# The low parts of the weights: VectorE alone in place of VectorE and GpSimd in turn

## What is computed

```
for l in range(2):                       # first network
    h = x @ w_in[l]                      # 1024 x 3620
    y = [mla(h), stick_breaking(h), forgetting(h), memory(h, mem @ w_mem_kv[l])]
    merged = sum(sigmoid(merge_r @ w_up[n]) * ((y[n] * silu(gate[n])) @ w_branch[l, n]))
    x = layer_norm(ALPHA * x + merged @ w_out[l])
for l in range(2):                       # second network
    z = rmsnorm(x, norm_g[l]) @ w_in_2[l]
    o = [dense A, window B, neighbourhood C, differential D attention of z], each * silu(its gate)
    x = x + concat(o) @ w_out_2[l]
return rmsnorm(x, final_g)
```

## Time and profile before

| | us |
|---|---|
| median of 3 runs | 1549.19 (1547.57 to 1551.87) |
| the profiled execution | 1553.94 |
| span of its trace | 1552.0 |
| PE busy | 1423.3 (92%) |
| VectorE busy | 904.6 (58%) |
| ScalarE busy | 681.2 (44%) |
| GpSimd busy | 366.7 (24%) |

### The profile page before, as it was taken

One profiled execution on the slowest core, in us unless ns is written; L12 is line 12 of the kernel. 1 busy time (PEld: TensorE's weight loads), 2 busy tenths in 40 slices (PEclk: granted clock), 3 DMA queues, 4 the chain that ended last, 5 costly groups with the idle time before them and its releaser, 6 DMA issues.

```text
span 1552.0 us, 21224 instructions
## 1 busy us (share of the span) xinstructions
PE 1423.3 (92%) x8026; PEld 1097.0 (71%) x8026; DVE 904.6 (58%) x1705; ACT 681.2 (44%) x1477; POOL 366.7 (24%) x265
## 2 busy tenths in 40 slices
PE   7999898999989999999998699997999799997997
PEld 7757675877987576767788666665777656664776
DVE  4655437556672554484576565468655466568655
ACT  3544344555233554444552344335444444335443
POOL 2232121245231321222452111410001111310011
PEclk9999999999999999999999799999999899998999
DMA  6412620225333121211263323511213322511211
GB/s 225 109 29 85 158 68 28 62 61 204 109 136 82 29 82 55 82 35 56 67 224 85 93 54 68 116 55 48 93 64 96 82 63 60 116 55 48 96 62 54
DMA packets 191120, 131.72 MB, mean 85 GB/s; under 512 B 91436, under 2 KB 181164, under 8 KB 191020
## 3 DMA queue, kind: packets, MB, share of 16 engines
q1 hardware_dynamic: 179534, 112.29, 26.0%
q10 hardware_dynamic: 11486, 18.09, 3.6%
HBM read 118.03 MB, written 12.32 MB: 84 GB/s over the span
## 4 chain that ended last, share of the span: by engine, by line
PE 68%; DVE 18%; ACT 7%; issue 3%; DMA 2%; ACTq 1%; POOL 0%; DVEq 0%; POOLq 0%
PE pb L1399 18%; PE pb L1400 16%; PE pb L1401 16%; PE pb L1477 5%; PE pb L1421 5%; PE pb L1455 4%; ACT prob L1533 2%; DMA wr<-w_out 2%; ACT wh L1552 2%; ACT tmp L1533 1%; DVE wl L1861 1%; DVE scr L2151 1%; DVE xl L1868 1%; DVE small L2128 1%; PE pb L1439 1%
## 5 line engine op out<-in xcount | busy, mean ns | idle before, releaser
L2296 POOL TENSOR_TENSOR wl<-wr,wh 128x512 fp32r<-128x512 f32 x170 | 236.7, 1392 | 893.8 <-ACT wh L1552 890.1
L1399 PE MATMUL pb<-xh,wl 128*128 128x512 f32 (+1 forms) x832 | 354.0, 425 | 25.1 <-DVE xl L1868 21.9
L1400 PE MATMUL pb<-xl,wh 128*128 128x512 f32 (+1 forms) x832 | 323.6, 389 | 0.0
L1401 PE MATMUL pb<-xh,wh 128*128 128x512 f32 (+1 forms) x832 | 323.2, 388 | 0.0
L1861 DVE TENSOR_TENSOR wl<-wr,wh 128x512 fp32r<-128x512 f32 x200 | 162.9, 815 | 159.3 <-ACT wh L1552 159.0
L1399 PEld LDWEIGHTS pb<-xh,wl 128*128 128x128 f32 x832 | 164.0, 197 | 106.4 <-issue 54.1
L1552 ACT CAST wh<-wr 128x512 fp32r<-128x512 f32 x370 | 211.0, 603 | 50.2 <-PE pb L1401 42.8
L1401 PEld LDWEIGHTS pb<-xh,wh 128*128 128x128 f32 x832 | 163.5, 197 | 32.0
L1400 PEld LDWEIGHTS pb<-xl,wh 128*128 128x128 f32 x832 | 164.8, 198 | 24.3 <-issue 3.8
L1533 ACT ACTIVATE prob<-prob,small 128x512 f32<-128x512 f32 (+3 forms) x128 | 76.2, 597 | 153.0 <-DVE small L2105 143.6
L1455 PE MATMUL pb<-cst,prob 128*128 128x128 f32 x768 | 118.5, 276 | 24.4 <-ACT prob L1533 8.2
(11 more groups left out here) (196 smaller groups left out, 2449.9 us busy)
## 6 DMA issues: line engine op xcount, KB each, us to landing
wr<-w_in SPq DMA_DIRECT2D x39, 1024.0 KB, 5.1
wr<-w_in SPq DMA_DIRECT2D x48, 256.0 KB, 4.6
wr<-w_out SPq DMA_DIRECT2D x10, 1024.0 KB, 5.7
wr<-w_branch SPq DMA_DIRECT2D x48, 128.0 KB, 2.3
x<-prob SPq DMA_DIRECT2D x12, 512.0 KB, 2.6
wr<-w_out SPq DMA_DIRECT2D x48, 128.0 KB, 3.0
wr<-w_mem_kv SPq DMA_DIRECT2D x4, 1024.0 KB, 5.5
prob<-x ACTq DMA_DIRECT2D x2, 2048.0 KB, 10.3
```

What stands on the lines that cost most here:

```text
L1399: e.matmul(ps, ll, rh, start=start, stop=False)
L1400: e.matmul(ps, lh, rl, start=False, stop=False)
L1401: t = e.matmul(ps, lh, rh, start=False, stop=stop)
L2296: t = e.tensor_tensor(wl[:, j % 2, c0:c1], wr[:, j % 2, c0:c1], wh[:, j % 2, c0:c1].bitcast(F32), ALU.subtract)
```

## The change

The step `cast` on VectorE loses its condition that the chunk be even, and GpSimd's branch for odd chunks is taken out, with its semaphore. PE and SyncE wait for the last chunk on the one semaphore that is left. The instruction is the same, with the same tiles; GpSimd keeps its other work. Behind the first hunk the line numbers of the changed kernel are up to 12 smaller (1861 becomes 1858).

```diff
-            c = (upto - 1) // 512
-            w.wait_ge(w_lo, w_lo.at((j, c - c % 2)))
-            if c:
-                w.wait_ge(w_lo2, w_lo2.at((j, c - 1 + c % 2)))
+            w.wait_ge(w_lo, w_lo.at((j, (upto - 1) // 512)))
...
-            elif k == "cast" and s["c"] % 2 == 0:
+            elif k == "cast":
...
-            elif k == "cast" and s["c"] % 2:
-                j, c = s["j"], s["c"]
-                c0, c1 = 512 * c, min(512 * c + 512, WEIGHTS[j][1] * WEIGHTS[j][2])
-                own()
-                w.wait_ge(w_hi, w_hi.at((j, c)))
-                t = e.tensor_tensor(wl[:, j % 2, c0:c1], wr[:, j % 2, c0:c1], wh[:, j % 2, c0:c1].bitcast(F32), ALU.subtract)
-                t.then_inc(w_lo2.sem, w_lo2.mark((j, c)))
...
-                    w.wait_ge(w_lo, w_lo.at((j - 2, c - c % 2)))
-                    w.wait_ge(w_lo2, w_lo2.at((j - 2, c - 1 + c % 2)))
+                    w.wait_ge(w_lo, w_lo.at((j - 2, c)))
```

More of the change, by code:

```diff
@@ L1229, in build @@
     w_lo, a_lo, v_copy, v_att, v_turn, v_fn = (signal(n) for n in ("w_lo", "a_lo", "v_copy", "v_att", "v_turn", "v_fn"))
-    w_lo2, y_lo, p_fn = (signal(n) for n in ("w_lo2", "y_lo", "p_fn"))
+    y_lo, p_fn = (signal(n) for n in ("y_lo", "p_fn"))
     (d_cst, d_tail, d_mem, d_pos, d_par, d_lam, d_z, d_spread, d_res, d_store, d_tab) = (
@@ L1241, in build @@
     SIGNALS = [feat, gemm, logit, turned, heado, aux, w_hi, a_hi, a_copy, a_att, a_turn, a_fn, w_lo, a_lo, v_copy, v_att,
-               v_turn, v_fn, w_lo2, y_lo, p_fn, d_cst, d_tail, d_mem, d_pos, d_par, d_lam, d_z, d_spread,
+               v_turn, v_fn, y_lo, p_fn, d_cst, d_tail, d_mem, d_pos, d_par, d_lam, d_z, d_spread,
                d_res, d_store, d_tab, *d_first, d_par1, *d_x, *d_w, *d_acc, *d_bias]
@@ L2280, in own @@
         def own():
-            w.wait_ge(w_lo2, w_lo2.n)
             w.wait_ge(y_lo, y_lo.n)
```

## The result

| | us | ratio to before (95% interval) |
|---|---|---|
| before, median of 6 runs | 1549.73 (1547.57 to 1552.42) | |
| changed, median of 6 runs | 1559.53 (1554.64 to 1564.57) | 1.006 (1.0035 to 1.0086) |
| changed, the profiled execution and its span | 1561.69, 1559.6 | |

A forecast was written before the change was run, and what follows sets the result against it. PE, busy 1423.3 of 1552.0 us, was taken as the bound, so only its stops count. Terms at known stops sum to plus 3.6 us, new stops add 2: 1549.2 + 5.6 = 1554.8, taken as 1555 us, range 1542 to 1571.

The forecast's parts named there:

- VectorE's work: VectorE's busy time: 904.6 us plus 102 for 170 moved rests, less 49 for collisions, gives 958 us.
- The relief: On VectorE, collisions with GpSimd's rests go: 29 us in the rests and 20 us in other instructions.
- Standing in line: On VectorE, a moved rest waits for ScalarE's cast and delays everything behind it; branch D's copy starts 2.2 us late.
- Branch D's sum: Branch D: 1.1 us late less 0.85 for a collision, about plus 0.25 per layer, bounds minus 1.5 and plus 2.2.
- Branch B: Rotations in branch B, second network: PE also waits for ScalarE, plus 0.9 us twice, 1.8.
- My term for new stops: PE stops not yet in the trace, where its lead is used up: 2 us, ends 0 and 12.
- First network and layer norm: Moved rests before PE's stops at latent and stick-breaking attention add time; collisions gone in layer 1's norm and merge save it.
- Rotations: Second network, PE's wait for line 2197: a moved rest stands right ahead, plus 0.3 us four times, 1.2.
- Relief wins: Rival: VectorE's collisions lie where PE stops, 12.8 us against 4 us of added cost, so 1540 us; chance 0.14.
- absorbed: Rival: the planner's lead swallows both added work and relief, so 1549 to 1552 us; chance 0.19.
- No relief: Rival: GpSimd does not slow VectorE, so 0.6 us is added everywhere, plus 15, 1564 us; chance 0.05.
- Lockstep: Rival: lateness spreads between VectorE and ScalarE through attention stages, plus 18 to 30, 1567 to 1579 us; chance 0.12.

The follow-up runs named there:

- two kernels that differ in it: Kernel without odd rests, TensorE reading high parts, 1522.98 us; the same with 170 odd rests made on GpSimd but not waited for by TensorE, 1547.38 us.
- the pair of traces above: Traces of the changed kernel and of it with 18 second-network rests put behind the next copy or mixing, which measured 1549.24 us, ratio 1.0001 to before.
- second_net: Against the kernel before, odd rests moved to VectorE in the second network only, left on GpSimd in the first: 1558.05 us, ratio 1.0050.
- the half kernel: Against the kernel before, odd rests moved to VectorE in the first network only, left on GpSimd in the second: 1553.70 us, ratio 1.0018.

## Why the prediction was right, point by point

- **VectorE's work.** Forecast 904.6 + 102 - 49 = 958 us; measured 961.5. The relief alone, from two kernels that differ in it, is 55.7 us against my 49; so the moved rests add some 112.6 (56.9 + 55.7) and not 102, and the two errors partly cancel. The mean of the rests was to be near 0.69 and is 0.755: GpSimd's other 86 additions and subtractions collide too; one rest in branch B took 2.47 us. I had said that those collisions stay, and did not look for what would newly stand beside them.
- **Standing in line, the mechanism.** Right, and in branch D right in size on VectorE. The copy was to start 2.2 us late: 2.25 (4.65 against 2.40). The next maxima 1.3 late: they start 8.05 us after the last ones (1071.98 - 1063.93) instead of 6.72. The stop behind line 1830 was to lose 0.85: it fell from 1.6 to 0.8.
- **Branch D's sum.** Wrong, plus 0.25 per layer. The failing step is "1.1 late where PE stands 3.1 us at 1084": I followed the delay only to stops that were in the trace already, by way of ScalarE's exponentials. PE also waits for this copy to leave its bank. Before, the copy ended 0.68 us ahead of the products (1067.62 against 1068.30), now 0.15 ahead, so only 0.53 us of its 2.25 were covered and 1.72 went into the stop. The upper bound that I gave, 2.2, held the stop (1.73 longer) but not the clock behind it; the place costs 4.70 against the kernel with the rest moved. Against the kernel before, PE loses 1.2 us over the whole of branch D in the first layer and 2.0 in the second, where I had 0.25. Some of it returns, because PE arrives later at the stop for the exponentials, 2.1 us at the longest now against 3.1.
- **Branch B.** I had plus 0.9 twice for the rotation. What was found is a new stop of 1.95 us ahead of the value products and, in this trace, the lower clock behind it: PE loses 3.6 and 3.5 us against the kernel before in the two layers. My term for new stops, 2 us with 12 as its end, was to hold all such places; two in B and two in D make up the loss of the second network (12.4 us in the pair of traces above, 8.3 by the medians). The term was mis-sized: by the medians it should have been some 4 us (8.3 less the 4.3 of my other terms for this network), by the traces up to 8 (3.6 + 3.5 + 1.2 + 2.0, less my 1.8 and 0.5 for these branches).
- **First network and layer norm.** My terms for it (latent 1.2, one at 174 of 0.6, stick-breaking 1.0, norm -1.9, merge -1.6) sum to -0.7; measured +3.9, with an interval of 0.2 to 5.4, so a gain of 0.7 is out and the size is open. The stops behind the latent attention grew by 2.8 (line 1474 behind ScalarE's copy, 7.3 to 10.1) where I had 1.2. The norm did not gain: its three rows of waits sum to 13.6 us (6.2 + 4.9 + 2.5), against 8.9 behind line 2080 and 4.3 behind 2072 before.
- **Rotations.** Right: 1.9 to 3.2 us at line 1505, forecast plus 1.2.
- **Rivals.** Relief wins and absorbed are out by the time. No relief had 1564, as far from the 1559.53 as the forecast; what puts it out are the rows, with the rests at 755 ns and the 55.7 us. Absorbed was not far from what the work can do: with 18 rests in another place the whole change is. Lockstep's mechanism, a late copy that makes PE late, was at work in four places, not in sixteen.

So the sign and the mechanism of standing in line were right, and the size, 5.6 against 9.8, was short in two places: in the stops that did not exist yet, with the clock behind them, and in the first network, where -0.7 stands against a measured 3.9 that no trace shows. Part of it is luck. The range, 1542 to 1571, would have held absorbed and no relief too, and 2 of the 5.6 us were a guess with no place named, while the terms that had a place were too low in branch D and branch B.

## What to carry to other kernels

Work that nobody waits for is only free on an engine that runs in order if nothing urgent stands behind it: look at what follows it, and at which bank or tile the next matmul needs back, before you look at the engine's share. When such work moves to another engine, put it there behind the next thing that PE waits for; 18 of 370 places decided here. And price a new stop of PE with the clock of the microseconds behind it, not with its length alone: in branch D the clock cost more than the stop, in branch B it fell in one trace and not in the other.

## What the hardware showed that was not expected

- A stop of 3.05 us was followed by granted clocks of 0.64 and 0.51 in the windows from 1068 to 1076, while one of 1.32 us at the same place left it at 1.00. In branch B it is 0.75 and 0.82 behind a stop of 1.95 us, and 1.00 behind a stop of 2.00 us in `second_net`. I draw no rule from these few.
- 170 subtractions of 1.29 us on GpSimd, 24% busy and hardly waited for, cost the kernel 24.4 us even with no wait for them left.
- The slow first stretch of one trace looked like part of a gain of 5.5 us; the time of the half kernel showed no gain.
